# The order of the score passes of an attention, in a kernel for one transformer and RWKV-7 layer

## Chip, core and metric

The kernel runs on one core of one Trainium2 chip. The core has five engines, each with a queue of its own: TensorE (PE) for matrix products, VectorE (DVE), ScalarE (ACT), GpSimd (POOL) and SyncE (SP), which here only issues transfers. They meet through semaphores alone. The metric is the device time of one launch in microseconds, as the median of several runs.

## The reference

One layer of a diffusion backbone on 512 latent tokens and 128 context tokens: a modulated norm, an input projection, attention beside a bidirectional RWKV-7 recurrence, an output projection, then an MLP. The change lies in the attention, which in the reference is

```python
keys = jnp.concatenate([_apply_rope(k, cos, sin), ctx_k.astype(k.dtype)], axis=2)
vals = jnp.concatenate([v, ctx_v.astype(v.dtype)], axis=2)
...
s = jnp.einsum("bkgqd,bkld->bkgql", qblk, k).astype(jnp.float32) * scale
p = jax.nn.softmax(s, axis=-1).astype(v.dtype)
return jnp.einsum("bkgql,bkld->bkgqd", p, v)
```

with 8 heads of width 64, two heads of keys and values, 512 latent queries against 768 keys (512 of their own and 256 cached), and 128 context queries against the 128 context keys.

## The kernel before

The phases run one after the other: the input projection with its gates, the first half of the recurrence (`chunks(0)`), the attention, the second half (`chunks(1)`), the branch and output projections, the MLP. A barrier (`phase_over(..., 2)`) stands between the attention and `chunks(1)`. Each engine's program is written out by hand, so that the order of the work is that of the Python loops; nothing schedules it.

The attention computes every score twice. In the **row pass**, `row_scores(n)` for n = 0 to 31 (8 heads of 4 tiles of 128 queries, L1042 on PE) forms 128 queries x 768 keys in one of three PSUM buffers (1.5 banks each, banks 0 to 5). DVE takes the negative maximum of each row (`score_max`, L2027), ACT the exponential with its sum (`row_exponentials`, L1552), and then the buffer is free: row n waits for exponential n - 3 (`rexp_done`). Maximum and logarithm of the sum give each query's log-sum. In the **key pass**, twelve ticks z of four blocks (L1084, L1085), the scores are formed once more with keys on the partitions, less the log-sum, which rides along as rows 64 to 127 of the second operand `q2` (`q_and_lse`); ACT's exponential (L1590) then gives finished weights, and `values` (L1108) multiplies them with the values one tick later.

The log-sums come from the columns to the rows of `q2` by a chain over three engines: `denominator_logs` (ACT, Ln, which needs another activation table than Exp), `lse_columns` (DVE, four small instructions), `lse_turn` (PE, into PSUM), `lse_row(h)` (DVE, one for each head). Before, this runs in two halves: the first 16 of 32 sums after row 20 on ACT, row 23 on DVE and row 26 on PE, the other half in the first ticks of the key pass, which starts with heads 0 to 3.

Between the rows lies the attention of the 128 context queries, in banks 6 and 7: `context_rows` (PE, n = 2), `context_diagonals` (DVE: two maxima, two diagonal matrices), `context_scores` (PE, n = 5: the maxima by a product with ones, then the scores on top), two exponentials (ACT, n = 7), `context_values` (PE, n = 9: weighted values into bank 6 and sums into bank 7), four reciprocals (`denominators`, DVE, n = 11 to 14) and `context_out` (DVE, n = 15).

Both passes also carry pieces of the preparation of `chunks(1)`: `between_heads(i)`, on PE `prepare_product` (L1011, also in banks 6 and 7), on ACT `key_squares`, `second_key_log` and `second_key_norm` (Ln and Exp again) and more, on DVE a generator that goes on by one step at a time. `head_ticks(z)` gives each tick its two or three pieces.

## Time and profile before

| | us |
|---|---|
| median of 3 runs | 1347.14 |
| lowest and highest | 1342.29, 1347.84 |
| the profiled execution, its device time | 1347.49 |
| its span | 1345.7 |
| PE busy in it | 1275.1 (95%) |
| DVE, ACT busy | 699.1, 552.0 |
| the row pass, from its first product to the first of the key pass | 445.59 to 500.82 |
| the key pass, to the first product behind it | 500.82 to 572.63 |

The profile is one execution. A group of instructions is named by its line, its engine, its operation and "out<-in". A duration is that of one instruction from issue to end. PE takes the next product before the last has ended, so that products started behind each other overlap and the step from start to start is shorter than a duration. "Idle before" is what an engine stood still ahead of an instruction, and behind the arrow stands what released it. PEclk is the granted TensorE clock as a share of 2.4 GHz.

### The profile page before, as it was taken

To read this page: it belongs to the slowest core of one execution; us is meant where nothing else is said; L and a number is where in the kernel's file an instruction comes from. 1 tells how busy PE (TensorE), PEld (TensorE's weight loads), DVE (VectorE), ACT (ScalarE), POOL (GpSimd) and SP (SyncE) were. 2 spreads that over 40 slices of the span, in tenths; PEclk is the share of its full clock that TensorE was granted. 3 is DMA by queue.
4 is the path that set the end of the run, shared out by engine and by line. 5 is a ranking of instruction groups with operands and counts; after the bars stand their busy time and mean duration, and the time that the engine had idled before them with its cause. 6 is when DMAs were issued, how large, how long until landed. Compare 5 with 4: busy or idle time off the path is not lost.

```text
span 1345.7 us, 31881 instructions
## 1 busy us (share of the span) xinstructions
PE 1275.1 (95%) x13903; PEld 1175.7 (87%) x13903; DVE 699.1 (52%) x1135; ACT 552.0 (41%) x922; POOL 41.2 (3%) x79
## 2 busy tenths in 40 slices
PE   4999999999999879899999999899999999999996
PEld 2899999999999554399989878799999999999995
DVE  4338643644544775565556412655554655533544
ACT  5445534432332576533342221733433334333433
POOL 0100011000010000000000000000000000000000
PEclk9999999999999988999999999999999999999998
DMA  9423375313400200010016494022121221022222
GB/s 387 157 73 109 108 275 188 102 50 98 125 4 4 94 1 0 1 54 17 27 42 251 180 366 180 26 80 83 62 94 62 66 90 39 24 78 75 70 73 94
DMA packets 26667, 131.58 MB, mean 98 GB/s; under 512 B 3232, under 2 KB 4000, under 8 KB 18240
## 3 DMA queue, kind: packets, MB, share of 16 engines
q1 hardware_dynamic: 21744, 103.94, 22.2%
q0 software_dynamic: 4816, 26.02, 5.2%
q8 instruction: 90, 1.47, 0.5%
q14 instruction: 17, 0.14, 0.0%
HBM read 111.67 MB, written 18.28 MB: 97 GB/s over the span
## 4 chain that ended last, share of the span: by engine, by line
PE 87%; DVE 5%; ACT 4%; DMA 2%; issue 1%; PEld 0%; PEldq 0%; DVEq 0%; ACTq 0%; SPq 0%
PE ps L718 47%; PE ps L1241 11%; PE ps L897 4%; PE ps L885 4%; PE ps L865 2%; PE ps L1108 2%; PE ps L753 1%; PE ps L877 1%; PE ps L743 1%; PE ps L1011 1%; PE ps L762 1%; DMA adaw<-in_wada 1%; DMA adl<-in_wada 1%; DVE nmax L2027 1%; PE ps L921 1%
## 5 line engine op out<-in xcount | busy, mean ns | idle before, releaser
L718 PE MATMUL ps<-h2lo,whi 128*128 128x320 f32 x672 | 153.3, 309 | 0.7 <-ACT facc L1348 0.7
L718 PE MATMUL ps<-h2hi,whi 128*128 128x320 f32 x672 | 153.1, 309 | 0.0
L718 PE MATMUL ps<-h2hi,wlo 128*128 128x320 f32 x672 | 153.0, 309 | 0.0
L1703 DVE TENSOR_TENSOR wlo<-raw,whi 128x2048 fp32r<-128x2048 f32 x47 | 107.5, 2287 | 72.9 <-ACT whi L1304 72.9
L718 PE MATMUL ps<-hlo,whi 128*128 128x320 f32 x544 | 126.8, 314 | 1.0 <-ACT qkv L1374 1.0
L718 PE MATMUL ps<-hhi,whi 128*128 128x320 f32 x544 | 124.0, 309 | 0.0
L718 PE MATMUL ps<-hhi,wlo 128*128 128x320 f32 x544 | 123.9, 309 | 0.0
L718 PEld LDWEIGHTS ps<-h2lo,whi 128*128 128x128 f32 x672 | 112.3, 188 | 1.0 <-DVE wlo L1703 1.0
L718 PEld LDWEIGHTS ps<-h2hi,wlo 128*128 128x128 f32 x672 | 112.5, 188 | 0.0
L718 PEld LDWEIGHTS ps<-h2hi,whi 128*128 128x128 f32 x672 | 112.3, 188 | 0.0
L1765 DVE SCALAR_TENSOR_TENSOR facc<-fraw,par,facc 128x512 f32<-128x512 f32 x88 | 44.6, 549 | 122.3 <-ACT facc L1348 122.3
L1347 ACT ACTIVATE fraw<-ps 128x512 f32<-128x512 f32 x88 | 33.7, 437 | 169.3 <-PE ps L718 168.1
L1304 ACT ACTIVATE whi<-raw 128x2048 fp32r<-128x2048 f32 x47 | 90.2, 1918 | 17.3 <-PE ps L718 11.6
L718 PEld LDWEIGHTS ps<-hlo,whi 128*128 128x128 f32 x544 | 90.9, 188 | 4.2 <-issue 2.4
L718 PEld LDWEIGHTS ps<-hhi,whi 128*128 128x128 f32 x544 | 90.9, 188 | 0.0
L718 PEld LDWEIGHTS ps<-hhi,wlo 128*128 128x128 f32 x544 | 90.9, 188 | 0.0
L1241 PE MATMUL ps<-dlo,whi 128*128 128x320 f32 x344 | 78.6, 309 | 3.7 <-DVE dlo L2182 2.5
L1241 PE MATMUL ps<-dhi,whi 128*128 128x320 f32 x344 | 78.2, 308 | 0.0
L1241 PE MATMUL ps<-dhi,wlo 128*128 128x320 f32 x344 | 78.2, 308 | 0.0
L2181 DVE TENSOR_TENSOR wlo<-raw,whi 128x512 fp32r<-128x512 f32 x44 | 30.4, 691 | 82.5 <-ACT dhi L1649 82.5
L1910 DVE COPY_PREDICATED tm<-con,ps 128x256 f32<-128x256 int32 x80 | 35.6, 445 | 64.7 <-PE ps L897 63.7
L1648 ACT ACTIVATE whi<-raw 128x512 fp32r<-128x512 f32 x44 | 27.8, 631 | 93.4 <-PE ps L1241 91.4
(351 smaller groups left out, 2586.2 us busy)
## 6 DMA issues: line engine op xcount, KB each, us to landing
raw<-in_wblk SPq DMA_DIRECT2D x48, 1024.0 KB, 4.9
adl<-in_wada SPq DMA_DIRECT2D x8, 2048.0 KB, 8.1
raw<-in_wdn SPq DMA_DIRECT2D x44, 256.0 KB, 2.6
adaw<-in_wada SPq DMA_DIRECT2D x4, 2048.0 KB, 21.2
gate_scratch<-gout POOLq DMA_DIRECT2D x16, 320.0 KB, 2.5
gld<-gate_scratch POOLq DMA_DIRECT2D x8, 640.0 KB, 4.9
attention_inputs_used<-attention_scratch SPq DMA_DIRECT2D x16, 316.0 KB, 3.1
u_scratch<-uout POOLq DMA_DIRECT2D x12, 320.0 KB, 2.4
```

The lines of the kernel that those rows point to most:

```text
L718: mm = pe.matmul(o, w, v, start=first, stop=last and w is hi and x is xh[n])
L865: mm = pe.matmul(bank(b, P, P * (2 * d + q))[r], src[r, d, tokens(d, q)], ar[s][r, d, chunk_of(g, d, q), :, :].rearrange("p a n -> p (a n) ...
L885: mm = pe.matmul(bank(b1, CH, CH * (2 * d + q))[r], abm[s][g % 2][r, d, q, 0, :], tm[s][r, d, q, :], start=True, stop=True)
L897: mm = pe.matmul(bank(b0, CH, CH * (2 * d + q))[r], left, right, start=True, stop=True)
L1241: mm = pe.matmul(o, w, v, start=(k == 0 and q == 0), stop=(k == FF - 1 and q == 2))
L1304: ac.activation(whi[s][:, :], raw[s][:, :], ACT.Copy).then_inc(hi_done, 1)
L1347: ac.activation(fr[j][:, at + 1:at + 1 + w], tile(2 * j)[:, a:a + w], ACT.Copy)
L1648: ac.activation(whi[0][:, 512:1024] if second else whi[s][:, 0:512], raw[s][:, 0:512], ACT.Copy)
L1703: TT(wlo[s][:, :], raw[s][:, :], whi[s][:, :].bitcast(F32), ALU.subtract).then_inc(lo_done, 1)
L1765: ins = STT(fa[j][:, a:a + w], fr[j][:, at:at + w], taps(0), fa[j][:, a:a + w], ALU.mult, ALU.add)
L1910: ins = dv.copy_predicated(t1[:, :, :, :], lev[:, l - 1].unsqueeze(2).broadcast_to(each), steps_of(bank(b0, 4 * CH)))
L2181: TT(wl, raw[s][:, 0:512], wh.bitcast(F32), ALU.subtract)
```

## The change

Nothing is computed differently. What changes is the place of the work in each engine's program, and the log-sums are handled once for all heads.

- The context attention moves back and is cut: its rows to n = 20, one maximum and diagonal each to n = 22 and 23 on DVE, the product of each maximum to n = 25 and 27 and the scores to n = 26 and 28 on PE, the exponentials to n = 28 and 29 on ACT, and its values behind the last row. There the sums (bank 7) come first, with a semaphore of their own.
- The two key products move from n = 16 and 20 to n = 12 and 15, their copies on DVE from 17 and 21 to 13 and 17; the squares on ACT from 11 (both) to 8 and 10.
- One `denominator_logs`, one `lse_columns` and one `lse_turn`, behind the last row, instead of two each. Both `second_key_log` stand right behind the one logarithm; `second_key_norm` goes between the first exponentials of the key pass.
- On DVE the reciprocals, `lse_columns`, `lse_row` of heads 0 and 1 and `context_out` stand behind the last row in this order; the other `lse_row` in the ticks 0 to 2.
- The first product of the preparation in the key pass (`between_heads(4)`) waits for `context_out`.

ACT, the row pass and the start of the key pass, before (L1552 the exponential of a row, L1573 of the context, L1396 the squares, L1561 and L1566 logarithm and norm of the keys, L1556 the logarithm of the sums):

```order
L1552 ACTIVATE ps,den<-ps,nmax 128x768 x8
L1573 ACTIVATE pt_123<-ps 128x512
L1573 ACTIVATE pt_124<-ps 128x512
L1552 ACTIVATE ps,den<-ps,nmax 128x768 x4
L1396 ACTIVATE tb_0_160<-uc_136,par 128x640
L1396 ACTIVATE tb_8_168<-uc_137,par 128x640
L1552 ACTIVATE ps,den<-ps,nmax 128x768 x9
L1561 ACT_TABLE_LOAD
L1561 ACTIVATE tb_1_161<-tb_1_161 128x640
L1556 ACTIVATE log_den<-den 128x16
L1566 ACT_TABLE_LOAD
L1566 ACTIVATE tb_1_161<-tb_1_161 128x640
```

and after, the end of the rows (L1549, L1572, L1553, L1558, L1563 are the same five; L1586 the exponential of the key pass):

```order
L1549 ACTIVATE ps,den<-ps,nmax 128x768 x18
L1572 ACTIVATE pt_123<-ps 128x512
L1549 ACTIVATE ps,den<-ps,nmax 128x768
L1572 ACTIVATE pt_124<-ps 128x512
L1549 ACTIVATE ps,den<-ps,nmax 128x768 x2
L1553 ACT_TABLE_LOAD
L1553 ACTIVATE log_den<-den 128x32
L1558 ACTIVATE tb_1_161<-tb_1_161 128x640
L1558 ACTIVATE tb_8_168<-tb_8_168 128x640
L1586 ACT_TABLE_LOAD
L1586 ACTIVATE pt_123<-ps 128x512
L1563 ACTIVATE tb_1_161<-tb_1_161 128x640
```

The table loads have left the rows; of four (the other two stood in tick 0) two are left, behind the last row.

DVE, rows 22 to 31 before (L2027 a row's maximum, L2034 to L2040 `lse_columns`, L2046 `lse_row`):

```order
L2027 TENSOR_REDUCE nmax<-ps 128x1 x2
L2034 TENSOR_TENSOR neg_lse<-nmax,log_den 128x16
L2035 CAST lse_hi<-neg_lse 128x16
L2039 COPY lse_columns<-lse_hi 128x4x4
L2040 TENSOR_TENSOR lse_columns<-neg_lse,lse_hi 128x4x4
L2027 TENSOR_REDUCE nmax<-ps 128x1 x4
L2046 TENSOR_SCALAR q_and_lse_131<-ps,con 64x512
L2027 TENSOR_REDUCE nmax<-ps 128x1 x2
L2046 TENSOR_SCALAR q_and_lse_132<-ps,con 64x512
L2027 TENSOR_REDUCE nmax<-ps 128x1 x2
```

and the last rows after (L2021 the maximum, L2043 a reciprocal, L2027 to L2031 `lse_columns`, L2037 `lse_row`, L2068 `context_out`):

```order
L2021 TENSOR_REDUCE nmax<-ps 128x1 x8
L2043 RECIPROCAL pt_124<-ps 128x128 x3
L2027 TENSOR_TENSOR neg_lse<-nmax,log_den 128x32
L2028 CAST lse_hi<-neg_lse 128x32
L2030 COPY lse_columns<-lse_hi 128x4x8
L2031 TENSOR_TENSOR lse_columns<-neg_lse,lse_hi 128x4x8
L2043 RECIPROCAL pt_124<-ps 128x128
L2037 TENSOR_SCALAR q_and_lse_131<-ps,con 64x512
L2037 TENSOR_SCALAR q_and_lse_132<-ps,con 64x512
L2068 TENSOR_TENSOR qc<-ps,pt_124 128x512
```

Three reciprocals now stand ahead of the log-sums, and nothing but maxima in the last eight rows.

PE after, from the last product of row 31 to the first of the key pass (L1056 row scores, L1123 context values, L1064 `lse_turn`, L1087 and L1088 the key pass); before, L1084 followed on row 31 directly:

```order
L1056 MATMUL ps<-attention_inputs_used,q_and_lse_132 128x256
L1123 MATMUL ps<-pt_123,attention_inputs_used 64x256
L1123 MATMUL ps<-pt_124,attention_inputs_used 64x256
L1123 MATMUL ps<-pt_123,attention_inputs_used 64x256
L1123 MATMUL ps<-pt_124,attention_inputs_used 64x256
L1123 MATMUL ps<-pt_123,attention_inputs_used 64x256
L1123 MATMUL ps<-pt_124,attention_inputs_used 64x256
L1123 MATMUL ps<-pt_123,attention_inputs_used 64x256
L1123 MATMUL ps<-pt_124,attention_inputs_used 64x256
L1064 MATMUL ps<-con,lse_columns 64x128 x4
L1087 MATMUL ps<-attention_inputs_used 128x512
L1088 MATMUL ps<-q_and_lse_131,attention_inputs_used 128x512
```

The context's eight products and the one turn now stand between the passes.

The diff, cut to its core:

```diff
@@ PE
@@ between_heads
-                    pe.wait_ge(lse_rows, 4)
+                    pe.wait_ge(o_copied, 1)
@@ lse_turn, now without half and bank: once, into bank 5
-            pe.wait_ge(lse_done, half + 1)
+            pe.wait_ge(rexp_done, 32)
+            pe.wait_ge(lse_done, 1)
@@ context_rows
+            pe.wait_ge(prep_read, 14)
@@ context_values: sums first
-            for b, a in ((6, 64), (7, 0)):
+            for b, a, made in ((7, 0, c_den_done), (6, 64, pv_done)):
...
         for n in range(32):
             row_scores(n)
-            if n == 2:
-                context_rows()
-            if n == 5:
-                context_scores()
-            if n == 9:
-                context_values()
-            if n == 16:
-                pe.wait_ge(o_copied, 1)
-                between_heads(2)
-            if n == 20:
-                between_heads(3)
-            if n == 26:
-                pe.wait_ge(prep_read, 14)
-                lse_turn(0, 6)
+            if n in (12, 15):
+                between_heads(2 + (n - 12) // 3)
+            if n == 20:
+                context_rows()
+            if n in (25, 27):
+                context_maxima((n - 25) // 2)
+            if n in (26, 28):
+                context_scores((n - 26) // 2)
+        context_values()
+        lse_turn()
         for z in range(12):
...
-            if z == 2:
-                lse_turn(1, 5)
@@ ACT, 32 rows
-            if n == 7:
+            if n in (8, 10):
+                key_squares(1, ((n - 8) // 2,))
+            if n in (28, 29):
+                p = n - 28
...
-            if n == 11:
-                between_heads(1)
-            if n == 20:
-                second_key_log(0)
-                denominator_logs(0)
-                second_key_norm(0)
+        denominator_logs()
+        for q in range(2):
+            second_key_log(q)
@@ ACT, key pass
+                if m < 2:
+                    second_key_norm(m)
-            if z == 0:
-                denominator_logs(1)
-                second_key_log(1)
-                second_key_norm(1)
@@ DVE, 32 rows
-            if n == 2:
-                context_diagonals()
-            if 11 <= n < 15:
-                denominators(n - 11)
-            if n == 15:
-                context_out()
-            if n in (17, 21):
-                s = (n - 17) // 4
+            if n in (13, 17):
+                s = (n - 13) // 4
...
-            if n == 23:
-                lse_columns(0)
-            if n in (27, 29):
-                lse_row((n - 27) // 2)
-        for h in (2, 3):
+            if n in (22, 23):
+                context_diagonals(n - 22)
+        for i in range(3):
+            denominators(i)
+        lse_columns()
+        denominators(3)
+        for h in range(2):
             lse_row(h)
+        context_out()
@@ DVE, key pass
-            if z == 1:
-                lse_columns(1)
-            if z in (2, 3):
-                for h in range(2 * z, 2 * z + 2):
+            if z < 3:
+                for h in range(2 * z + 2, 2 * z + 4):
                     lse_row(h)
```

## Rows read from the trace of the kernel before

**Rows 1.** Busy time by stretch: us, busy of each engine, PEclk, DMA, GB/s.

```profile
445.60:500.80 55.20, 41.91 (x196) 30.32 (x197) 39.75 (x52) 34.53 (x69) 0.00 (x0) 0.90 0.16 58
500.80:515.90 15.10, 12.44 (x35) 6.10 (x33) 9.00 (x19) 12.31 (x20) 0.00 (x0) 0.73 0.00 0
```

**Rows 2.** Timeline, one turn of three rows: start us, us, engine, line, idle before.

```profile
458.30 2.69 DVE L2027 TENSOR_REDUCE nmax<-ps 128x1 f32<-128x768 f32 x3 [2.15 <-PE ps L1055]
...
459.30 0.88 ACT L1552 ACTIVATE ps<-ps,nmax 128x768 f32<-128x768 f32 x1 [2.08 <-DVE nmax L2027]
...
460.34 0.50 PE L1054 MATMUL ps<-attention_inputs_used 128*128 128x512 f32 x1 [0.67 <-ACT ps L1552]
```

**Rows 3.** Timeline of PE: starts of rows, and what stands between.

```profile
445.59 0.47 PE L1054 MATMUL ps<-attention_inputs_used 128*128 128x512 f32 x1 [1.87 <-DVE rwo L1993]
...
450.48 0.50 PE L1054 MATMUL ps<-attention_inputs_used 128*128 128x512 f32 x1 [1.24 <-ACT ps L1552]
...
462.19 3.63 PE L1118 MATMUL ps<-pt,attention_inputs_used 128*64 128x256 f32 x16 [0.89 <-ACT pt L1573]
...
490.12 0.79 PE L1054 MATMUL ps<-attention_inputs_used 128*128 128x512 f32 x1 [4.12 <-ACT ps L1552]
...
499.58 0.59 PE L1054 MATMUL ps<-attention_inputs_used 128*128 128x512 f32 x1 [0.81 <-ACT ps L1552]
...
500.82 0.63 PE L1084 MATMUL ps<-attention_inputs_used 128*128 128x512 f32 x1
```

**Rows 4.** Timeline of DVE: context, copy and log-sums.

```profile
450.95 1.28 DVE L2070 TENSOR_REDUCE nmax<-ps 128x4 f32<-128x512 f32 x2
452.27 1.29 DVE L2074 TENSOR_TENSOR pt<-con,nmax 128x512 f32<-128x512 f32 x2
...
468.50 0.95 DVE L2052 RECIPROCAL pt<-ps 128x128 f32<-128x128 f32 x1
...
480.51 0.81 DVE L2093 COPY tb<-ps 128x640 f32<-128x640 f32 x1
...
496.75 0.76 DVE L2046 TENSOR_SCALAR q_and_lse<-ps,con 64x512 fp32r<-64x512 f32 x1
...
506.55 0.17 DVE L2034 TENSOR_TENSOR neg_lse<-nmax,log_den 128x16 f32<-128x16 f32 x1 [2.09 <-ACT log_den L1556]
```

**Rows 5.** Timeline of PE: the pieces that move.

```profile
453.04 1.10 PE L1091 MATMUL ps<-pt,onesr 128*128 128x512 f32 x2
454.07 1.16 PE L1094 MATMUL ps<-qc,attention_inputs_used 64*128 64x128 f32 x8
...
482.48 1.02 PE L1011 MATMUL ps<-tb,con 128*128 128x512 f32 x2
...
493.73 1.09 PE L1062 MATMUL ps<-con,lse_columns 128*64 128x128 f32 x8
```

**Rows 6.** Timeline of ACT: the pieces that move.

```profile
461.06 1.08 ACT L1573 ACTIVATE pt<-ps 128x512 f32<-128x512 f32 x2
...
469.52 1.54 ACT L1396 ACTIVATE tb<-uc,par 128x640 f32<-128x640 f32 x2
...
505.01 1.28 ACT L1556 ACT_TABLE_LOAD   x1
506.31 0.21 ACT L1556 ACTIVATE log_den<-den 128x16 f32<-128x16 f32 x1
```

**Rows 7.** Busy time and PEclk around three waits.

```profile
485.90:489.70 3.80, 0.10 (x1) 0.00 (x0) 2.50 (x7) 3.76 (x6) 0.00 (x0) 0.99 0.01 2
489.70:492.90 3.20, 2.78 (x9) 2.40 (x10) 0.96 (x1) 2.23 (x7) 0.00 (x0) 0.50 0.00 0
...
510.10:516.80 6.70, 6.70 (x14) 2.50 (x15) 4.60 (x9) 3.44 (x6) 0.00 (x0) 0.50 0.00 0
458.30:461.30 3.00, 2.33 (x12) 1.66 (x10) 2.69 (x3) 2.00 (x5) 0.00 (x0) 1.00 0.00 0
```

**Rows 8.** Timeline of PE: a wait in the second tick of the key pass.

```profile
509.94 1.97 PE L1011 MATMUL ps<-wdad,hpw 64*128 64x512 f32 x2 [2.66 <-ACT tb L1418]
```

More of the change, by code:

```diff
@@ L454, in build @@
     q2_zero, c_rows_done = sem("zeros_below_q"), sem("context_row_scores")
+    c_den_done = sem("context_denominators")
     st_done, exp_done, pv_done, rden_done, o_copied = (
@@ L1056, in row_scores, with lse_turn @@
             mm.then_inc(row_s_done, 1)
-        def lse_turn(half, b):
-            pe.wait_ge(lse_done, half + 1)
+        def lse_turn():
+            pe.wait_ge(rexp_done, 32)
+            pe.wait_ge(lse_done, 1)
             for qt in range(4):
-                mm = pe.matmul(bank(b, P, P * qt)[64:128], lse_cols[:, qt, :], ident, start=True, stop=True)
+                mm = pe.matmul(bank(5, P, P * qt)[64:128], lse_cols[:, qt, :], ident, start=True, stop=True)
             mm.then_inc(lse_turned, 1)
@@ L1086, in key_scores, with context_maxima, context_scores @@
                     .then_inc(st_done, 1)
-        def context_scores():
-            for p in range(2):
-                pe.wait_ge(diag_done, 1 + p)
-                pe.matmul(bank(6 + p), onesr[:, :].bitcast(F32), cdiag[p].rearrange("p t n -> p (t n)"), start=True, stop=False)
-                rows = slice(64 * p, 64 * p + 64)
-                for j in range(4):
-                    mm = pe.matmul(bank(6 + p, P, P * j), k2c_u[rows, j // 2, :], qc[rows, j, :], start=False, stop=j == 3)
-                mm.then_inc(st_done, 1)
+        def context_maxima(p):
+            pe.wait_ge(diag_done, 1 + p)
+            pe.matmul(bank(6 + p), onesr[:, :].bitcast(F32), cdiag[p].rearrange("p t n -> p (t n)"), start=True, stop=False)
+        def context_scores(p):
+            rows = slice(64 * p, 64 * p + 64)
+            for j in range(4):
+                mm = pe.matmul(bank(6 + p, P, P * j), k2c_u[rows, j // 2, :], qc[rows, j, :], start=False, stop=j == 3)
+            mm.then_inc(st_done, 1)
         def values(u, c):
@@ L1119, in context_values @@
                                        pt[p][:, 5, 256 * g:256 * g + 256], start=True, stop=True)
[L1120 removed]
+                mm.then_inc(made, 1)
         pe.wait_ge(q2_ld, 128)
@@ L1391, in low_tanh, with key_squares @@
             ac.activation(gdT[:, :], gdT[:, :], ACT.Tanh, scale=0.5).then_inc(low_done, 1)
-        def key_squares(it):
-            for s in range(2):
+        def key_squares(it, pairs=range(2)):
+            for s in pairs:
                 ac.wait_ge(rw_ld[it][s], 32)
@@ L1535, in between_heads @@
         def between_heads(i):
-            if i == 1:
-                key_squares(1)
-            elif i >= 5:
+            if i >= 5:
                 e, k = (i - 5) // 6, (i - 5) % 6
@@ L1552, in row_exponentials, with denominator_logs @@
             ac.activation(out, out, ACT.Exp, bias=nmax[:, n:n + 1], accum_out=den[:, n:n + 1]).then_inc(rexp_done, 1)
-        def denominator_logs(half):
-            ac.wait_ge(rexp_done, 16 * half + 16)
-            ac.activation(lnd[:, 16 * half:16 * half + 16], den[:, 16 * half:16 * half + 16], ACT.Ln).then_inc(lnd_done, 1)
+        def denominator_logs():
+            ac.wait_ge(rexp_done, 32)
+            ac.activation(lnd[:, :], den[:, :], ACT.Ln).then_inc(lnd_done, 1)
         def second_key_log(s):
@@ L1569, in _ @@
             row_exponentials(n)
-            if n == 7:
-                for p in range(2):
-                    ac.wait_ge(st_done, 1 + p)
-                    ac.activation(pt[p][:, 5, :], bank(6 + p), ACT.Exp).then_inc(exp_done, 1)
-            if n == 11:
-                between_heads(1)
-            if n == 20:
-                second_key_log(0)
-                denominator_logs(0)
-                second_key_norm(0)
+            if n in (8, 10):
+                key_squares(1, ((n - 8) // 2,))
+            if n in (28, 29):
+                p = n - 28
+                ac.wait_ge(st_done, 1 + p)
+                ac.activation(pt[p][:, 5, :], bank(6 + p), ACT.Exp).then_inc(exp_done, 1)
+        denominator_logs()
+        for q in range(2):
+            second_key_log(q)
         for s in range(2):
```

40 lines of the change are left out of this document (17 added, 23 removed).

## Prediction

> **What bounds the kernel now.** I read the busy times by stretch first [rows 1]. From the first row to the first product of the key pass PE is busy for 41.9 of 55.2 us, DVE for 39.8 and ACT for 34.5: no engine is full. In the next stretch, 15.1 us for the first two ticks of the key pass, PE counts as busy for 12.4, but at a PEclk of 0.73. So the row pass is bound by waits between engines, and the first two ticks by a wait and a slow clock.
>
> What a row costs when nothing else runs is in the timeline [rows 2]. Three rows turn in three buffers: the maxima start at 458.30, the first exponential at 459.30, PE refills that buffer at 460.34. PE needs 0.96 for a row and DVE starts again at 461.34: a turn takes 3.04 us for three rows, 1.013 us each. In a turn DVE works for 2.6 (three maxima of 0.87, one behind another), ACT for 2.65 (0.88 each), PE for some 2.1 from start to start (2.33 by durations, which overlap [rows 7]), 0.70 a row: gaps of 0.43, 0.39 and 0.94 in which a piece of other work fits. The 31 steps from the first row to the start of the last would take 31 x 1.013 = 31.4 us.
>
> They take 499.58 - 445.59 = 54.0 us [rows 3]. Of the 22.6 too many, 1.85 go at the start (4.89 to row 3 in place of 3.04, since DVE is still busy with the recurrence). The rest belongs to the pieces. The dearest are the values of the context (3.63 behind a wait of 0.89, for 16 products at half clock) and the logarithm amid the rows (PE idle for 4.12 us). The context's rows, maxima and scores, four reciprocals one after each of four rows, the wait for `context_out` and the half clock behind such waits make up the others.
>
> **The change, term by term** (against the profiled execution, 1347.5 us; the median is 0.35 below it).
>
> *A, the first row to the start of the last.* The start stays: 1.85. Pieces left in the rows, each less the gap of its engine in its turn:
> - two copies on DVE, 0.81 - 0.43 each [rows 4]: 0.8; both context maxima with their diagonals in one turn, 1.28 + 1.29 - 0.43 [rows 4]: 2.1;
> - two squares on ACT, 1.54 - 0.39 [rows 6]: 1.1;
> - the key products on PE, 1.2 each (1.02 for the two long parts and the short ones behind them) less 0.94 [rows 5]: 0.5; the context rows (as many short products as two score groups at 1.16 would have eight each; in a row's shadow I take 1.16 - 0.94): 0.2;
> - maxima and scores, 2 x (1.10 + 1.16) = 4.5, over rows 25 to 28, less a turn and a third of gap [rows 5]: 3.3; the two exponentials (1.08 for both) [rows 6] beside it: 0.
>
> Together 8.0; since pieces of different engines share turns I take 7.5. A = 31.4 + 1.85 + 7.5 = 40.8 in place of 54.0: **-13.2**. Bounds: only the maxima, scores and diagonals show, 5.4 (A = 38.7, -15.3); every piece in full, 1.6 + 2.6 + 1.5 + 1.1 + 2.4 + 1.2 + 4.5 = 14.9 (A = 48.2, -5.8).
>
> *B, from the start of the last row to the key pass.* Now 500.82 - 499.58 = 1.24, nothing between [rows 3]. After, a chain that nothing covers: the last row through three engines 3.0; ACT comes late to it by the second context exponential, 0.6; table and logarithm 1.28 + 0.21 [rows 6], at 5.1. Meanwhile PE needs about 1.0 for the first half of the context's values (full clock, half of 3.63 / 2), starts it at 2.0, and the three reciprocals behind it (3 x 0.86, one behind another, 0.95 for one) [rows 4] keep DVE until 5.7, so they end later than the logarithm. Then `lse_columns` 4 x 0.17, the turn 1.09, one `lse_row` 0.76 and some 0.3 for four handovers: 8.6. B = **+7.4**. Bounds: +6.1 if DVE waits for no reciprocal and ACT is not late; +9.5 if the values and the turn run at half clock and ACT is later.
>
> *C, the first two ticks.* Now 15.05. The logarithm, the log and the norm of the second key with their two tables are gone from the end of tick 0, so the wait of 2.66 for L1418 goes [rows 8]. That leaves 12.4 us. PE enters them, as now, after some microseconds with little to do. Before, such a wait (0.10 busy in 3.8 us) was followed by 3.2 us at 0.50, and the wait of 2.66 by 6.7 us at 0.50 [rows 7]. So I keep the clock of now and take 12.0. C = **-3.0**. Bounds: full clock all along, 12.44 busy x 0.73 = 9.1 [rows 1] (-6.0); or the two norms between the first exponentials cost PE 1.5, about their 2 x 0.77 as the like squares [rows 6]: 13.5 (-1.5).
>
> *D, later.* The second turn and its lines are gone from tick 2 (at most 1.09 of PE), but later ticks wait for ACT anyway: **-0.4**, between 0 and -0.9. The barrier and all behind it move up unchanged: the transfers there hang on the barrier or on later work.
>
> What is moved past what: the squares at rows 8 and 10 read operands that SP loads during the first rows; before they came at 469.5 [rows 6], now from about 458.5. No transfer runs from 458.30 on [rows 7]. I cost this at nothing. `between_heads(4)` waits for `context_out`, last of DVE's block (0.7 behind two `lse_row`), while PE has eight products of the key pass to do: nothing.
>
> Sum: -13.2 + 7.4 - 3.0 - 0.4 = -9.2, so 1338.3 against the profiled time and **1338.0** as a median. With all bounds at their low ends (-15.3 + 6.1 - 6.0 - 0.9 = -16.1) it would be 1331, with all at their high ends (-5.8 + 9.5 - 1.5 = +2.2) 1349.3.
>
> The table load in the chain is 1.28 by its row, and the logarithm follows it at once [rows 6]. The Trainium skill ("ScalarE: Activation LUTs", What ACT_TABLE_LOAD costs) gives the same 1283 ns but adds 1380 ns of drain, 2.66 us for each switch. By that rule the chain would be 1.4 longer, the sum 1.4 less; the row has no such gap, and I go by the row.
>
> **The rivals.**
>
> 1. *The pieces show in full.* The turn of three rows is bound by latency, and a piece may hit a row that is due instead of a gap. Against it: with three buffers, a delay on one engine is partly taken up by the gaps of the two others. For it: the row that waits for a reciprocal waits for all of its 0.95 [rows 4]. A = 48.2, and the sum is -5.8 + 7.4 - 3.0 - 0.4 = -1.8: 1345.3.
>
> 2. *The one long wait costs the clock more than two short ones.* PE has the eight products of the context's values, the turn and nothing else in some 8 us. If the clock falls inside it, values and turn run at half clock (B = +9.5), and the first two ticks hardly gain (C = -1.5): -13.2 + 9.5 - 1.5 - 0.4 = -5.6, 1341.5. For it: PEclk 0.50 behind both waits [rows 7]. Beside this stands the Trainium skill ("TensorE: Matmul & The Clock Gate", HAM oscillation), by which waits between short bursts throttle PE each time, which speaks against gathering waits in one place only if that place is long; the trace agrees that a wait of 3.8 us is enough.
>
> 3. *The clock holds.* If the key pass starts at full clock, C = -6.0 and the sum is -12.2, with the pieces in their gaps (A = -15.3) -14.3. Between these: 1334.
>
> 4. *Slower: PE falls to half clock in the rows.* With the context gone from the first 20 rows PE works for 2.1 of 3.04 us there. At half clock a row costs PE twice its 0.70, 1.40, which is over 1.013, so PE would bind. If this held for all 31 steps: 31 x 0.39 = 12.1, and the pieces of PE (2.4 + 1.2 + 4.5) would cost twice, 8.1 more: -9.2 + 20.2 = +11.0, 1358.2. It turns slower than before from about half of the rows on. Against it: the turn of [rows 2] has 2.33 busy of 3.00 us and a PEclk of 1.00 [rows 7], and a stretch at half clock is itself full of work, and the one behind 489.7 ended at 492.9.
>
> **How the numbers follow.** The forecast gets 0.62 (its own range 1334 to 1341.5), rival 1 0.14, rival 2 0.12, rival 3 0.08, rival 4 0.04. The bounds on A and C are wide, so the range is 1333 to 1345: it leaves out rival 4, half of 1 and a part of 3, under 0.2. What a measurement can tell from no change is about 0.5%, 6.7 us: faster means below 1340.4. That holds nine tenths of the forecast (0.56), rival 3 (0.08) and a third of rival 2 (0.04): 0.68. Slower is rival 4 and a little: 0.05. The rest, 0.27, is the same.
>
> **What the profile after should show.** The last row starts 40.8 us behind the first (38.7 to 48.2); between rows no idle time of PE near 4 us. DVE: three reciprocals, then `lse_columns` with no wait for ACT. The first product of the key pass 8.6 us behind the start of the last row, at a PEclk of 0.50. The third tick 12.0 behind that, with no wait of PE for ACT's L1417 in the second. No activation table loaded in the rows. The forecast is wrong if the rows take over 45 us (rival 1), if PEclk is low in them (rival 4), or if the ticks from the third on take longer than before, which I have no term for: every wait on ACT there stands the same in both programs.

## The result, and the profile after

| | before | after |
|---|---|---|
| median of 12 runs each, us | 1347.44 | 1339.38 |
| lowest and highest | 1341.07, 1352.50 | 1335.85, 1341.62 |
| profiled execution; its span | 1347.49; 1345.7 | 1340.27; 1338.5 |

The ratio is 0.9944 with an interval of 0.9930 to 0.9957: 7.5 us or 0.56% faster. The forecast was 1338.0.

The stretches of the prediction in the two profiles, with E for all that lies behind the barrier:

| stretch, us | before | after | change | foreseen |
|---|---|---|---|---|
| A, first row to start of the last | 53.99 | 39.84 | -14.15 | -13.2 |
| B, from there to the first product of the key pass | 1.24 | 8.57 | +7.33 | +7.4 |
| C, two ticks | 15.05 | 12.70 | -2.35 | -3.0 |
| D, third tick to the barrier | 56.76 | 55.40 | -1.36 | -0.4 |
| E, barrier to the end of the span | 773.07 | 776.41 | +3.34 | 0 |

The last row starts at 485.42 in after. PE, timeline of after: start, us, what, idle before with its releaser; it answers to [rows 3, 5]:

```profile
445.58 0.47 PE L1055 MATMUL ps<-attention_inputs_used 128*128 128x512 f32 x1 [1.86 <-DVE rwo L1987]
...
450.47 0.50 PE L1055 MATMUL ps<-attention_inputs_used 128*128 128x512 f32 x1 [2.56 <-ACT ps L1549]
...
485.42 0.40 PE L1055 MATMUL ps<-attention_inputs_used 128*128 128x512 f32 x1
...
487.45 1.95 PE L1123 MATMUL ps<-pt,attention_inputs_used 128*64 128x256 f32 x16 [1.17 <-ACT pt L1572]
...
491.92 1.06 PE L1064 MATMUL ps<-con,lse_columns 128*64 128x128 f32 x8 [2.52 <-DVE lse_columns L2031]
...
493.99 0.76 PE L1087 MATMUL ps<-attention_inputs_used 128*128 128x512 f32 x1 [1.01 <-DVE q_and_lse L2037]
...
506.69 0.50 PE L1087 MATMUL ps<-attention_inputs_used 128*128 128x512 f32 x1
```

Between the rows PE stands still for at most 0.67 us, but for the one wait of 2.56 ahead of row 3. The wait of 4.12 [rows 3] is gone; in its place come three behind the last row. What they wait for stands on DVE and on ACT, timelines of the same execution (they answer to [rows 4] and [rows 6]):

```profile
488.58 2.58 DVE L2043 RECIPROCAL pt<-ps 128x128 f32<-128x128 f32 x3 [0.97 <-PE ps L1123]
491.08 0.13 DVE L2027 TENSOR_TENSOR neg_lse<-nmax,log_den 128x32 f32<-128x32 f32 x1
...
491.68 0.95 DVE L2043 RECIPROCAL pt<-ps 128x128 f32<-128x128 f32 x1
493.08 1.43 DVE L2037 TENSOR_SCALAR q_and_lse<-ps,con 64x512 fp32r<-64x512 f32 x2 [0.45 <-PE ps L1064]
```

```profile
486.81 0.59 ACT L1572 ACTIVATE pt<-ps 128x512 f32<-128x512 f32 x1
487.29 0.87 ACT L1549 ACTIVATE ps<-ps,nmax 128x768 f32<-128x768 f32 x1
488.07 0.21 ACT L1549 ACTIVATION_READ_ACCUMULATOR ps<-ps,nmax 128x1 f32 x1
488.16 0.88 ACT L1549 ACTIVATE ps<-ps,nmax 128x768 f32<-128x768 f32 x1
...
489.18 1.28 ACT L1553 ACT_TABLE_LOAD   x1
490.47 0.23 ACT L1553 ACTIVATE log_den<-den 128x32 f32<-128x32 f32 x1
...
495.28 1.28 ACT L1586 ACT_TABLE_LOAD   x1 [3.32 <-PE ps L1088]
496.57 0.60 ACT L1586 ACTIVATE pt<-ps 128x512 f32<-128x512 f32 x1
```

As in the prediction, `neg_lse` waits for nothing of ACT: the logarithm ends at 490.70, the third reciprocal at 491.16. The clock, by stretch (us, busy time with counts of PE, PEld, DVE, ACT and POOL, PEclk, DMA share, GB/s), answers to [rows 1, 7]:

```profile
452.00:456.00 4.00, 4.00 (x16) 3.30 (x14) 3.15 (x4) 3.15 (x8) 0.00 (x0) 0.57 0.87 344
485.90:489.70 3.80, 2.33 (x19) 1.24 (x17) 2.83 (x4) 3.77 (x8) 0.00 (x0) 1.00 0.00 0
...
496.00:500.00 4.00, 4.00 (x9) 1.98 (x7) 2.14 (x3) 3.87 (x7) 0.00 (x0) 0.50 0.00 0
500.00:504.00 4.00, 4.00 (x10) 2.77 (x10) 3.07 (x5) 2.93 (x5) 0.00 (x0) 0.60 0.00 0
```

Two places run at or near half clock: a stretch of the rows behind the wait of 2.56, and the first ticks, as forecast. Behind the barrier 3.3 us came back. 0.8 of it lies in the second half of the recurrence. 2.2 lies from one block of the MLP's modulation to the next phase, timeline of after:

```profile
772.92 3.56 PE L754 MATMUL ps<-adl,silu_c 128*32 128x512 f32 x16 [2.06 <-DMA adl<-in_wada]
```

and the same block before:

```profile
782.15 1.92 PE L753 MATMUL ps<-adl,silu_c 128*32 128x512 f32 x16 [1.51 <-DMA adl<-in_wada]
```

Both wait for a transfer. The block starts 15.9 us behind the first block of its kind, in place of 15.4: 0.6 of the 2.2. Its 16 products take 3.56 in place of 1.92: 1.64, for the clock (PEclk 0.53 in 772.90 to 776.50, and before 1.00 in 782.10 to 784.10). The experiments say whether the change has to do with it.

### The profile page after: what moved, and what is told of

The parts are those of the page before. It is cut to its first block, busy times and chain, and to the rows that moved or that the text cites. A ratio compares the mean times of both kernels' runs of the same rounds, so it can differ in the third digit from the quotient of the medians.

```text
span 1338.5 us, 31858 instructions
## 1 busy us (share of the span) xinstructions
PE 1272.8 (95%) x13895; PEld 1174.8 (88%) x13895; DVE 699.2 (52%) x1131; ACT 549.7 (41%) x919; POOL 41.2 (3%) x79
## 4 chain that ended last, share of the span: by engine, by line
PE 88%; DVE 4%; ACT 3%; DMA 2%; issue 1%; PEld 0%; PEldq 0%; DVEq 0%; ACTq 0%; SPq 0%
PE ps L719 47%; PE ps L1240 11%; PE ps L898 4%; PE ps L886 4%; PE ps L866 2%; PE ps L754 2%; PE ps L1113 1%; PE ps L878 1%; PE ps L744 1%; PE ps L1012 1%; PE ps L763 1%; DMA adaw<-in_wada 1%; DMA adl<-in_wada 1%; PE ps L1087 1%; PE ps L922 1%
```

## The experiments

The theory at the outset: the gain is in the rows, since context and logarithms hit rows that were due; the chain B is a sum of durations, with DVE's reciprocals its longest branch; C is set by the clock at which PE comes out of the gap. The rivals: the chain is set by ACT; the ticks are set by the norms among ACT's exponentials; the +3.3 of E is caused by the change. The stretches of all kernels (the clock is PEclk in 452 to 456):

| kernel | clock | A | B | C | D | to the barrier | E | ratio to before, interval |
|---|---|---|---|---|---|---|---|---|
| before | 1.00 | 53.99 | 1.24 | 15.05 | 56.76 | 127.0 | 773.07 | |
| after | 0.57 | 39.84 | 8.57 | 12.70 | 55.40 | 116.5 | 776.41 | 0.9944, 0.9930-0.9957 |
| changed_again | 0.50 | 40.90 | 8.56 | 12.81 | 55.47 | 117.7 | 773.55 | 0.9951, 0.9932-0.9971 |
| one_turn_only | 1.00 | 45.27 | 8.41 | 10.67 | 57.12 | 121.5 | 773.07 | 0.9992, 0.9970-1.0014 |
| one_turn_again | 1.00 | 48.39 | 8.43 | 10.52 | 57.08 | 124.4 | 775.51 | 0.9989, 0.9973-1.0006 |
| cols_first | 0.58 | 39.84 | 8.68 | 12.65 | 55.41 | 116.6 | 776.79 | 0.9923, 0.9899-0.9946 |
| cols_one | 1.00 | 39.21 | 8.27 | 10.40 | 57.08 | 115.0 | 776.29 | 0.9951, 0.9937-0.9966 |
| log_later | 1.00 | 39.17 | 9.54 | 9.92 | 55.45 | 114.1 | 773.32 | 0.9938, 0.9916-0.9960 |
| context_block | 0.57 | 40.63 | 8.99 | 10.24 | 55.50 | 115.4 | 774.74 | 0.9942, 0.9923-0.9961 |
| context_sooner | 0.77 | 40.26 | 7.54 | 9.89 | 55.47 | 113.2 | 777.28 | 0.9938, 0.9920-0.9956 |
| busy_between | 0.57 | 40.28 | 9.19 | 9.30 | 53.81 | 112.6 | 773.16 | 0.9927, 0.9898-0.9956 |
| first_parts_early | 1.00 | 39.18 | 8.57 | 14.03 | 55.44 | 117.2 | 777.22 | 0.9940, 0.9914-0.9966 |
| busy_row2 | 1.00 | 40.01 | 8.57 | 9.91 | 55.44 | 113.9 | 773.18 | 0.9934, 0.9911-0.9958 |
| all_filled | 1.00 | 39.52 | 7.53 | 9.05 | 57.02 | 113.1 | 773.20 | 0.9893, 0.9873-0.9913 |

Each row is one profiled execution; the ratio is from several.

### One half of the change alone

*one_turn_only* is the kernel before with the log-sums in one block; context and key pieces stay.

```diff
@@ PE
-            if n == 26:
-                pe.wait_ge(prep_read, 14)
-                lse_turn(0, 6)
+        lse_turn()
-            if z == 2:
-                lse_turn(1, 5)
@@ ACT
-            if n == 20:
-                second_key_log(0)
-                denominator_logs(0)
-                second_key_norm(0)
+        denominator_logs()
+        for q in range(2):
+            second_key_log(q)
@@ DVE
-            if n == 23:
-                lse_columns(0)
-            if n in (27, 29):
-                lse_row((n - 27) // 2)
-        for h in (2, 3):
+        lse_columns()
+        for h in range(2):
             lse_row(h)
```

> The kernel before with one part of the change alone: one logarithm, one set of columns, one turn for all heads behind the last row, and the logarithms and norms of the second keys there; the context and the key products stay in their old rows. My account of the change: out of the rows go the wait for the tables in the middle (PE idle 4.1, some 3.6 more than a turn), the half clock and the turn behind it (1.6) and two lse_row (1.0), so the rows to the start of the last take 54.0 - 6.2 = 47.8 us. The chain behind the last row has no context values and no reciprocals: 8.6 - 0.6 = about 8.0. The first two ticks take about 12.7, as in the changed kernel. Together about -3 us against before to the barrier, and some 7 us more than the changed kernel. Rival: the gathering of the log-sums is what pays and the place of the context hardly matters: then rows of about 41 to 43 us and the full gain of 10 us to the barrier.

The rows took 45.27, 2.5 less than expected, and the ticks 10.67. In time nothing: 0.9992. Two timelines of PE show the gap that took it back:

```profile
495.69 1.94 PE L1061 MATMUL ps<-con,lse_columns 128*64 128x128 f32 x8 [4.49 <-DVE lse_columns L2029]
...
498.64 0.77 PE L1083 MATMUL ps<-attention_inputs_used 128*128 128x512 f32 x1 [1.01 <-DVE q_and_lse L2035]
```

PE waits 4.49 at once here, and the turn behind it runs at half clock (1.94 in place of 1.06). *one_turn_again* is the same kernel once more, since the first profile was of the fastest of its ten executions.

> The kernel before with one log-sum for all heads behind the last row, once more, since its first profile was the fastest of its ten runs and stood 5.5 us below before to the barrier, while the median of the ten was 0.8 us below. If the log-sums' place is worth some 3 us by itself, the median is 1 to 4 us below before and the rows take 45.3 at full clock, up to 48 where the clock falls among the context's pieces; the chain is 8.4 again. If it is worth as much as the first profile showed, the median is 5 us below.

The rows now took 48.39, at a clock that falls twice (busy time by stretch; the first has 1.00 in the first of these stretches):

```profile
460.00:465.00 5.00, 3.60 (x18) 2.30 (x20) 2.12 (x3) 4.08 (x10) 0.00 (x0) 0.77 0.00 0
...
475.00:480.00 5.00, 3.96 (x10) 2.66 (x11) 2.23 (x4) 1.98 (x4) 0.00 (x0) 0.66 0.00 0
```

The 16 products of the context's values took 3.43 here and 1.95 there. One program, two executions, 3.1 us apart in A. To the barrier the single turn gains 5.5 or 2.6 us, and the rest of the change another 4 to 8 (to 116.5 or 117.7); the medians (1345.13 and 1345.71 beside 1345.96 and 1345.91 of before) give the first half no gain that can be told. The intervals leave it 4 us at most.

The record says where its gain went. These 22 executions had a mean granted clock of 0.9847, and the 61 of before in all four sets 0.9862. By a line fitted to the 61 (1.0 us for each 0.001), one_turn is some 2.5 us faster than before at the same clock, and the 18 executions of the changed kernel some 6.9. So the new place of the log-sums does save time, and the lower clock, as behind the wait of 4.49, takes about as much away. These are estimates from fitted lines. The second half of the change, the moves of the context and the key pieces, was not run alone.

### What ends the chain

*cols_first* takes the columns ahead of the reciprocals; with that ACT's logarithm alone holds them.

```diff
-        for i in range(3):
-            denominators(i)
         lse_columns()
-        denominators(3)
+        for i in range(2):
+            denominators(i)
         for h in range(2):
             lse_row(h)
+        for i in range(2, 4):
+            denominators(i)
```

> The changed kernel, DVE with the columns of the log-sums ahead of all four reciprocals, two reciprocals then and two behind the two lse_row. My account: the reciprocals end 0.4 us after the logarithm, so the chain from the last row to the key pass falls from 8.57 to about 8.2, no more, since ACT's logarithm at 490.7 is then what it waits for. Rows, ticks and time otherwise the same (within 0.5 us). Rival: the reciprocals stand in the way for their whole 2.6 us, then 8.57 falls to about 6.

It missed: 8.68. DVE, timeline:

```profile
491.39 0.19 DVE L2027 TENSOR_TENSOR neg_lse<-nmax,log_den 128x32 f32<-128x32 f32 x1 [3.12 <-ACT log_den L1553]
...
492.06 1.76 DVE L2043 RECIPROCAL pt<-ps 128x128 f32<-128x128 f32 x2
493.85 1.43 DVE L2037 TENSOR_SCALAR q_and_lse<-ps,con 64x512 fp32r<-64x512 f32 x2
```

The columns do start sooner, 5.3 behind the last row in place of 5.7, but the two reciprocals put under the turn need 1.76, and the `lse_row` behind them starts 0.5 after the turn has ended. I had moved the wait by one step. *cols_one* puts only one reciprocal there:

```diff
-        denominators(3)
+        denominators(0)
         for h in range(2):
             lse_row(h)
+        for i in range(1, 4):
+            denominators(i)
```

(and nothing ahead of `lse_columns`).

> The changed kernel, DVE with the columns first, one reciprocal while PE turns them, then the two lse_row, then the other three reciprocals. The first try of this kind had two reciprocals there (1.76 us), and they held up the lse_row by 0.5, more than it gained. One (0.95) fits in the 1.2 us of the turn. Expected: the chain at 8.2 (8.57 less the 0.4 by which the reciprocals were late), if ACT's logarithm is what comes next; no change (8.6) if something else holds it.

8.27, so 0.3 is what the reciprocals cost the chain. It is not a gain in full: `context_out`, now behind three reciprocals, holds PE's preparation product in the first tick for 1.62.

*log_later* lengthens the other branch by 1.35, by both logarithms of the keys ahead of that of the sums.

```diff
-        denominator_logs()
         for q in range(2):
             second_key_log(q)
+        denominator_logs()
```

> The changed kernel with the two logarithms of the keys (0.65 us each) ahead of that of the sums on ACT: a dose put into the chain. If the chain behind the last row is a plain sum with the reciprocals 0.4 us behind the logarithm, 1.3 us more on ACT make it 8.57 + 1.3 - 0.4 = 9.5. If the chain hung on DVE or PE alone, it stays at 8.6.

9.54. Timelines of DVE, of ACT and of PE; DVE now waits 0.82 for ACT:

```profile
491.54 0.19 DVE L2027 TENSOR_TENSOR neg_lse<-nmax,log_den 128x32 f32<-128x32 f32 x1 [0.82 <-ACT log_den L1553]
```

```profile
488.73 1.28 ACT L1558 ACT_TABLE_LOAD   x1
490.02 1.36 ACT L1558 ACTIVATE tb<-tb 128x640 f32<-128x640 f32 x2
491.29 0.21 ACT L1553 ACTIVATE log_den<-den 128x32 f32<-128x32 f32 x1
```

```profile
492.43 1.06 PE L1064 MATMUL ps<-con,lse_columns 128*64 128x128 f32 x8 [3.49 <-DVE lse_columns L2031]
```

A chain 1.0 longer, and yet PE reached the barrier 2.4 us sooner than in after, since its ticks took 2.8 and its rows 0.7 less. The clock outweighs the chain.

*context_sooner* moves the context's pieces two rows up, so that its second exponential no longer stands between those of rows 29 and 30.

```diff
-            if n in (25, 27):
-                context_maxima((n - 25) // 2)
-            if n in (26, 28):
-                context_scores((n - 26) // 2)
+            if n in (23, 25):
+                context_maxima((n - 23) // 2)
+            if n in (24, 26):
+                context_scores((n - 24) // 2)
@@ ACT and DVE likewise: exponentials n in (26, 27), diagonals n in (20, 21)
```

> The changed kernel with the context's pieces two rows sooner, so that its exponentials stand behind rows 26 and 27 on ACT and not ahead of the last two. By the account ACT came 0.6 us late to the last row because of them: the chain falls to about 8.0, the context values start with no wait, and the reciprocals are done ahead of the logarithm. Rows 39.2 at full clock behind row 2, 39.8 or more if not. If the 0.6 is DVE's or PE's, the chain stays at 8.6.

7.54, a larger gain than expected. The last row starts at 487.92 here; ACT and DVE, two timelines:

```profile
489.92 0.88 ACT L1549 ACTIVATE ps<-ps,nmax 128x768 f32<-128x768 f32 x1 [0.28 <-DVE nmax L2021]
...
492.22 0.23 ACT L1553 ACTIVATE log_den<-den 128x32 f32<-128x32 f32 x1
```

```profile
489.95 2.58 DVE L2043 RECIPROCAL pt<-ps 128x128 f32<-128x128 f32 x3
492.49 0.19 DVE L2027 TENSOR_TENSOR neg_lse<-nmax,log_den 128x32 f32<-128x32 f32 x1
```

The last exponential starts 2.00 behind the row's start, in place of 2.74 (488.16 - 485.42), and the reciprocals 2.03 in place of 3.16, because the values no longer wait for the late exponential. So both branches hung on that one piece, and B fell by 1.0. Not all of it need be a gain: the last row itself starts a little later in this order. all_filled, which has the same order at full clock, has an A of 39.52, where the others had 39.2; A and B together are 47.05 there and 47.75 in first_parts_early, 0.7 apart. `neg_lse` now starts (492.49) within 0.04 of the end of both, the logarithm's (492.45) and the reciprocals' (492.53).

*context_block* makes the context's pieces one behind another at 22, 25 and 28.

```diff
-            if n in (25, 27):
-                context_maxima((n - 25) // 2)
-            if n in (26, 28):
-                context_scores((n - 26) // 2)
+            if n == 25:
+                for p in range(2):
+                    context_maxima(p)
+                    context_scores(p)
@@ ACT: both exponentials at n == 28; DVE: both diagonals at n == 22
```

> The changed kernel with the context's pieces at the end of the rows in blocks and not cut: both maxima and diagonals at row 22 on DVE, both products of maxima and scores at row 25 on PE, both exponentials at row 28 on ACT. By my account a piece costs what is over the gap of its engine in its turn, so both diagonals in one place (2.6) cost as before, 2.1, but 4.5 us of PE in one turn cost 4.5 - 0.94 = 3.6 in place of 3.3: the rows take 0.3 to 1.0 us more (40.1 to 40.8), the chain 0.5 less to the same. If cutting is what pays, the rows lose 2 us or more.

A was 40.63, 0.8 over after and 0.3 under changed_again, and B 8.99, 0.4 over both; with the clock of its rows as low as theirs, little can be told from a single profile. The ratios (0.9942 and 0.9944) don't differ, and their intervals are some 2.5 us wide to each side. Whether the small pieces are better than blocks stays open.

### What sets the first ticks

*busy_between* adds 17 products on PE that nothing reads, 4 ahead of the context's values, 10 ahead of the turn and 3 behind it.

```diff
+        pe.wait_ge(rexp_done, 30)
+        keep_busy(4)
         context_values()
+        keep_busy(10)
         lse_turn()
+        keep_busy(3)
```

> The changed kernel with 17 products that nobody reads put on PE between the passes (4 ahead of the context values, 10 ahead of the turn, 3 behind it), 0.235 us each, in the time in which PE is idle. Rival 2 and term C say: the first two ticks cost 12.7 in place of 9.1 since PE comes to them at half clock. If the clock is the cause, PEclk stays near 1.00 from 492 to 504 and the two ticks take 9.1 to 9.7; the chain stays at 8.6 (up to 9.0 if a product more than fits stands ahead of the turn). The whole is 3 us faster than the changed kernel. If the ticks are slow for another reason (the two norms between the exponentials on ACT), they stay at 12 or more and the whole does not move.

B grew by 0.6, C fell to 9.30, the 9.1 of the prediction's bound. Busy time by stretch:

```profile
492.00:496.00 4.00, 3.88 (x20) 2.63 (x19) 3.48 (x9) 1.07 (x2) 0.00 (x0) 1.00 0.00 0
496.00:500.00 4.00, 4.00 (x15) 2.39 (x14) 1.91 (x4) 3.44 (x5) 0.00 (x0) 1.00 0.00 0
```

The norms and the table load on ACT are the same as in after, so they don't set C (12.70 there): the clock does. How long it is low is what differs: in busy_row2, where C is 9.91, PEclk is 0.78 in 492 to 496, 0.79 in the next 4 us and then 1.00, while after has 0.62, 0.50 and 0.60. The table load behind a wait of 3.32 (495.28, above) is exposed, but hides behind PE's products.

*first_parts_early* fills the gap with useful work: the first half of four key scores, which needs no log-sum, ahead of the turn.

```diff
+        for m in range(4):
+            pe.wait_ge(rexp_done, 30 if m < 2 else 31)
+            pe.matmul(bank(m), kst_u[:, 0, 0, m // 2 * P:m // 2 * P + P],
+                      qst_u[m % 2][:, 0, :], start=True, stop=False)
         lse_turn()
@@ key_scores
+                if m >= 4:
                     pe.matmul(out, ..., start=True, stop=False)
```

> The changed kernel with the first of the two products of the key pass's first four blocks issued between the context values and the turn, where PE waits; they do not read the log-sums. Real work, the same in sum. 4 x 0.43 us at half clock or 4 x 0.235 at full leave the first tick: -1.7 us if the clock still falls. Whether it falls, the two theories differ: if 0.94 us of work in a wait of 2.5 keeps the clock, the two ticks take about 8.5 (the gain is 4 us), if not about 11 (the gain is 1.7).

It missed both ways: 14.03.

```profile
492.00:496.00 4.00, 2.99 (x11) 1.65 (x10) 2.45 (x5) 1.51 (x2) 0.00 (x0) 0.69 0.02 4
496.00:500.00 4.00, 4.00 (x8) 2.45 (x9) 2.51 (x4) 4.00 (x8) 0.00 (x0) 0.50 0.00 0
500.00:504.00 4.00, 4.00 (x8) 2.02 (x8) 3.86 (x9) 2.05 (x4) 0.00 (x0) 0.50 0.00 0
```

The four products (1.20) did not hold the clock in this execution, and it stayed down for nearly the whole of both ticks. In *cols_one*, with less work in the gap, it held:

```profile
490.00:494.00 4.00, 1.43 (x10) 1.14 (x10) 2.83 (x7) 1.87 (x4) 0.00 (x0) 1.00 0.00 0
494.00:498.00 4.00, 2.38 (x9) 1.34 (x8) 3.93 (x7) 3.56 (x6) 0.00 (x0) 1.00 0.01 4
```

So a half-filled gap may go either way. The filled one held in both kernels that have it (busy_between and all_filled), in one profile of each.

*busy_row2* puts 9 unread products behind row 2, where PE waits for 2.56.

```diff
             row_scores(n)
+            if n == 2:
+                pe.wait_ge(rwo_done, 2)
+                for _ in range(9):
+                    pe.matmul(bank(7), kst_u[:, 0, 0, 0:P], qst_u[0][:, 0, :], start=True, stop=True)
```

> The changed kernel with nine products that nobody reads behind row 2. There PE stands still for 2.56 us since the context's rows left that place, and in five of eight profiles its clock was at half from 452 to 456, with rows of 39.8 to 40.9 us; in three it was full, with 39.2. If the wait is the cause, the clock stays full and the rows take 39.2; if it is chance in those profiles, PEclk in 452 to 456 may be 0.5 again.

The clock behind the wait was full, but the rows took 40.01. Busy time by stretch, then the timeline of PE:

```profile
446.00:449.50 3.50, 3.50 (x12) 3.00 (x13) 3.21 (x5) 0.00 (x0) 0.00 (x0) 0.57 0.84 218
...
452.00:456.00 4.00, 3.32 (x18) 2.61 (x17) 2.95 (x4) 2.91 (x7) 0.00 (x0) 1.00 0.98 388
```

```profile
449.55 2.41 PE L1134 MATMUL ps<-attention_inputs_used 128*128 128x512 f32 x9
451.80 0.39 PE L1055 MATMUL ps<-attention_inputs_used 128*128 128x512 f32 x1
```

The clock was low ahead of the wait already, which made rows 0 to 2 late. That alone costs nothing: cols_one and log_later had 0.60 and 0.57 in 446 to 449 too, their row 3 still started 4.88 behind row 0, and their rows took 39.2. Here the nine products started late behind the slow rows and stood in the way of row 3, which started 5.8 behind row 0, 0.9 late. So this filling cost some 0.8 us. Nor does it settle whether the wait is what lowers the clock at 452: cols_one and log_later had full clock there without any filling, and so had first_parts_early. The cause of the low clock in the other six stays open.

Across the table the rows of the changed order took 39.17 to 39.21 where the clock at 452 to 456 was full without help, and 39.84 to 40.90 where it was near half.

### Is what came back behind the barrier the change's doing?

*changed_again* is the changed kernel once more.

> The changed kernel itself once more, for a second execution of each stretch beside the experiments. If the stretches are set by the order of the work, the rows come again to 39.8 and the chain to 8.6 within 0.1, and so does everything that the clock does not touch; the first two ticks (12.7) and the time behind the barrier (776.4, against 773.1 in three of the six profiles so far) may differ by what the clock does. If instead the change itself made the time behind the barrier 3.3 us longer, it is 776.4 again.

To the barrier it is like the first, 1.2 later by A. Its E is 773.55, 2.9 shorter. Over all kernels E is 773.1 to 773.6 seven times, in before among them, and 774.7 to 777.3 seven times, in both of one program twice (after, one_turn). So it is no fixed cost of the change. Whether the change makes it more frequent isn't shown: E is high in six of the eleven profiles of the changed order and in one of the other three. D has such steps too: it comes as 53.8, 55.4 or 57.1 in all kernels but that of before, whose third tick is 1.34 longer (56.76 - 1.34 = 55.4). Ticks 6 and 9 of the key pass have a wait of PE for ACT's L1417 (1.45 in after), and the tick takes 6.7 us, or 7.8 to 8.4 when the clock falls in it. After, then changed_again, ticks 6 and 9 (busy time by stretch; the two were 6.70 and 7.77, then 8.36 and 6.72 long):

```profile
526.20:532.90 6.70, 5.25 (x23) 2.57 (x21) 5.88 (x12) 2.74 (x5) 0.00 (x0) 1.00 0.00 0
542.00:549.80 7.80, 6.35 (x23) 2.71 (x21) 5.25 (x10) 2.74 (x5) 0.00 (x0) 0.86 0.00 0
```

```profile
528.40:536.70 8.30, 6.86 (x22) 2.96 (x20) 6.03 (x12) 2.75 (x5) 0.00 (x0) 0.79 0.00 0
545.80:552.50 6.70, 5.26 (x22) 2.57 (x20) 5.09 (x10) 2.75 (x5) 0.00 (x0) 1.00 0.00 0
```

The times of whole executions agree with this. Over 22 executions of the kernel before, beside one_turn_only, the mean granted clock runs from 0.981 (1352.9 and 1354.3) to 0.990 (1342.7 and 1343.0), and the least-squares slope is 1.1 us for each 0.001, with a correlation of -0.92. The other sets of five or more that I fitted have slopes of 0.7 to 1.3.

### All that helped, together

*all_filled* has the context two rows sooner, the four first parts ahead of the turn, and unread products: 9 behind row 2, 6 ahead of the turn, 3 behind it.

```diff
+            if n == 2:
+                pe.wait_ge(rwo_done, 2)
+                for _ in range(9):
+                    pe.matmul(bank(7), ...)
@@ behind context_values: the four first parts, then
+        pe.wait_ge(rexp_done, 32)
+        for _ in range(6):
+            pe.matmul(bank(4), ...)
         lse_turn()
+        for _ in range(3):
+            pe.matmul(bank(4), ...)
@@ and the moves of context_sooner
```

> The changed kernel with four edits together: the context's diagonals, maxima, scores and exponentials two rows sooner (20, 23 to 26, 26 and 27); the first products of four blocks of the key pass between the context values and the turn; six products that nobody reads ahead of the turn and three behind it; nine such behind row 2, where PE waits 2.6 us for DVE. By the account: rows 39.2 (full clock all along); ACT is not late for the last row, so the chain falls from 8.6 to about 8.0; the first two ticks at full clock and without 0.94 us of their work 8.3; to the barrier 6 us less than the changed kernel's profile, and as a median 4 to 6 us less, about 1334. If the half clock only moves to another place, the two ticks stay over 10 and the median gains 1 or 2.

1331.40 (1329.67 to 1334.51): ratio 0.9893 (0.9873 to 0.9913), whose interval lies below that of after. It beats both kernels, the changed one by some 7 us (0.9893 against 0.9944). PEclk at its places:

```profile
452.00:456.00 4.00, 3.68 (x19) 2.73 (x17) 3.39 (x4) 3.71 (x9) 0.00 (x0) 1.00 1.03 407
...
492.00:496.00 4.00, 3.68 (x14) 1.89 (x13) 2.27 (x5) 1.99 (x3) 0.00 (x0) 1.00 0.00 0
496.00:500.00 4.00, 3.53 (x13) 1.72 (x12) 2.96 (x5) 4.00 (x8) 0.00 (x0) 1.00 0.00 0
```

Its five runs had a mean clock of 0.990 to 0.994, before's beside them 0.985 to 0.989. An execution of first_parts_early that happened to have 0.990 took 1334.22, one of all_filled with 0.990 took 1334.51. Over more executions there is a difference: by a line fitted to the 18 executions of the changed kernel, the five of all_filled are some 3 us faster at the same mean clock, an estimate, since the line has to be drawn on beyond their 0.991. So more than half of what this kernel gains over the changed one is that its clock is low less often, and the rest is the order.

## Why the prediction was right

The mechanism was right in the main, with exceptions in A and D, but that 1338.0 lies so near to 1339.4 is in part luck. To the barrier the profile gained 10.5 us (9.3 in changed_again), where the sum had 9.2: A and D gained 1.9 more than foreseen, C 0.6 less. Behind the barrier, which the sum held at nothing, this execution lost 3.3.

- **A** (-14.15; foreseen -13.2, bounds -15.3 to -5.8). The step "31 x 1.013 + 1.85 + 7.5" gave 40.8. Where the clock held, the rows took 39.2: the pieces showed with 5.9, not 7.5. In after the half clock added some 0.6, in changed_again 1.7. That is rival 4's mechanism for a few rows and not for 31. The wait of 1.24 ahead of row 3 [rows 3] became one of 2.56, since the context rows had left that gap, and I had counted their leaving as gain alone; that the longer wait is what lowers the clock isn't shown (busy_row2). Rival 1, 48.2, is refuted.
- **B** (8.57; foreseen 8.6). The form of the chain was right (its terms as written add to 8.5), and the reciprocals are its longest branch: 0.3 by cols_one, and from where ACT takes over by log_later. The prediction had them end at 5.7 and the logarithm at 5.1; they ended at 5.74 and 5.28. One term was mis-sized: the late exponential of the context, "0.6", made ACT 0.74 late, and its removal gave 0.7 to 1.0 (context_sooner, all_filled), because PE's values and with them the reciprocals start behind it too. Its low bound, 7.3 without either, is near that kernel's 7.54.
- **C** (-2.35; foreseen -3.0). The clock at the first ticks was low, as forecast, and the stretch is that of the forecast. But "I keep the clock of now" was a choice among cases, not a property of the kernel, and that the profile fell on it was luck: with the same work, C took 9.9 to 10.4 in five kernels with an unfilled gap (10.5 to 10.7 in one_turn), and 12.6 to 12.8 in both profiles of the changed kernel and one more. Full clock gave 9.3; the bound of 9.1 was good. The wait of 2.66 in the second tick [rows 8] is gone. Rival 2 had the clock fall inside the gap; the turn ran at full clock (1.06) in after, and at half in one_turn_only.
- **D** (-1.36; foreseen -0.4, bounds 0 to -0.9). This left its bounds. The third tick took 5.25 before and 3.90 to 3.94 in all the other kernels; the next three take the same 5.2 in before and after. So all of it is the third tick, where I had written that later ticks wait for ACT anyway. That one doesn't: from the turn to the next tick it takes 2.73 before and, with the values alone, 1.87 in after, so the turn showed with 0.86; and its first eight products take 2.52 in place of 2.04, 0.48 for a clock that was still low (PEclk 0.75 in 515.80 to 518.00).
- **E** (+3.3; foreseen 0). "All behind it moves up unchanged" holds for the work and not for the clock. It is no fixed effect of the change, but it is why the profile shows 7.2 us in place of the sum's 10.5. With the profile's own E of before, the time would have been 1337. The median, over 12 executions, has such clock losses on both sides: -8.1 by medians, -7.5 by the ratio.
- Table loads: in after the logarithm starts 1.29 behind the start of its load (489.18, 490.47), and the exponential likewise (495.28, 496.57). The Trainium skill's 1380 ns of drain for each switch ("ScalarE: Activation LUTs", What ACT_TABLE_LOAD costs) stands against the trace; the row was right.

## What to carry to other kernels

Where three engines pass rows round, take out of the rows what can stand alone, but look at what each piece filled: a wait that it covered is a place where TensorE's clock may fall. Small clock losses in a few places are worth as much here as a whole rearrangement, and filling waits with products that nothing reads, costing 0.6 us of chain, brought 0.6 to 3.4 us in the ticks behind. Filling that comes late costs: nine products behind rows at half clock held up the next row by 0.9. And when a change gains less than 1%, compare the mean granted clock of both sets of runs first, and judge a stretch by several executions.

## What the runs showed of the hardware

- The granted clock differs between executions of one program: at half or full at the same place, in 452 to 456, in ticks 6 and 9, and behind a wait for a transfer near 773. Each such place costs between 0.6 us (452 to 456 in after) and some 3 us (the first ticks). For all the kernel 0.001 of mean clock was about 1 us.
- The same gap doesn't always cost the clock: with 1.43 us of work in 4 us it stayed at 1.00 (cols_one), with 2.60 in 4 us it fell in the next 4 and was low for over 12 us (first_parts_early). The Trainium skill ("TensorE: Matmul & The Clock Gate", HAM oscillation) describes a kernel in which the wait for a transfer behind each short burst throttles TensorE every time. Here all but one of these waits are for other engines, and the same wait was followed by the low clock in some executions and not in others.
- A table load that stands ahead of an exponential starts only when that exponential's operand is there: ACT was idle for 3.32 us, and then loaded for 1.28 (2.56 and 1.28 in cols_one).
